# Query, key and value projections by Strassen's seven products over sequence, channel and column halves

## The reference

```python
def dilated_mixer(x, w_qkv, w_o, t5_table):                      # layer A
    qkv = (x @ w_qkv).reshape(B, S, N_DIL, 3, N_HEADS_A, HEAD_DIM)
...
def neighbourhood_mixer(x, w_qkv, w_o, rpb):                     # layer B
    qkv = (x @ w_qkv).reshape(B, rows, GRID_W, 3, H, Dh)
```

## Time and profile before

| | |
|---|---|
| median of 3 runs | 6017.46 us (6017.22 to 6020.44) |
| the profiled execution | 6019.97 us, span of its instructions 6018.3 us |
| TensorE (PE) busy | 5663.1 us, 94% |
| VectorE / ScalarE / POOL busy | 2881.3 / 2306.9 / 1227.2 us |
| mean granted TensorE clock | 0.967 of full speed |
| 16 DMA engines | 212 GB/s mean |

### The profile page before, as it was taken

One profiled execution on the slowest core, in us unless ns is written; L12 is line 12 of the kernel. 1 busy time (PEld: TensorE's weight loads), 2 busy tenths in 40 slices (PEclk: granted clock), 3 DMA queues, 4 the chain that ended last, 5 costly groups with the idle time before them and its releaser, 6 DMA issues. The chain is left out here.

```text
span 6018.3 us, 93104 instructions
## 1 busy us (share of the span) xinstructions
PE 5663.1 (94%) x29818; PEld 4768.2 (79%) x29819; DVE 2881.3 (48%) x5557; ACT 2306.9 (38%) x4179; POOL 1227.2 (20%) x910
## 2 busy tenths in 40 slices
PE   8999999999899997879999979998999896999997
PEld 6888888888799996768887837887999785888773
DVE  3222232222255557675866552322444455755785
ACT  1111111111177775445655411112666213655571
POOL 1331100000000000054755320000000002634673
PEclk9999999999999998979999979999999897999998
DMA  8767744433499987477888574443444325876987
GB/s 252 228 222 234 232 139 138 137 119 119 127 321 316 311 252 209 137 260 261 324 300 297 207 277 153 136 123 118 142 129 136 118 92 183 307 264 224 348 307 276
DMA packets 590506, 1275.30 MB, mean 212 GB/s; under 512 B 39838, under 2 KB 204365, under 8 KB 590220
## 3 DMA queue, kind: packets, MB, share of 16 engines
q1 hardware_dynamic: 398908, 738.28, 36.7%
q0 software_dynamic: 77200, 294.76, 14.1%
q10 hardware_dynamic: 114112, 238.41, 13.1%
HBM read 941.32 MB, written 348.87 MB: 214 GB/s over the span
## 5 line engine op out<-in xcount | busy, mean ns | idle before, releaser
L519 DVE SCALAR_TENSOR_TENSOR qa_stage_lo<-qa_ps_out,qa_stage 128x512 fp32r<-128x512 f32 x192 | 132.5, 690 | 1110.1 <-ACT qa_stage L442 1098.8
L406 PE MATMUL qa_ps_out<-qa_xT_hi,qa_w_hi 128*128 128x512 f32 x1536 | 598.9, 390 | 0.0
L406 PE MATMUL qa_ps_out<-qa_xT_lo,qa_w_hi 128*128 128x512 f32 x1536 | 598.7, 390 | 0.0
L406 PE MATMUL qa_ps_out<-qa_xT_hi,qa_w_lo 128*128 128x512 f32 x1536 | 598.5, 390 | 0.0
L442 ACT ACTIVATE qa_stage<-qa_ps_out 128x512 fp32r<-128x512 f32 x192 | 114.8, 598 | 931.3 <-PE qa_ps_out L406 931.3
L1775 POOL TENSOR_TENSOR a_ex_w_lo<-a_ex_w_raw,a_ex_w_hi 128x1024 fp32r<-128x1024 f32 x128 | 352.8, 2788 | 132.2 <-ACT a_ex_w_hi L1772 127.9
L1775 POOL TENSOR_TENSOR b_ex_w_lo<-b_ex_w_raw,b_ex_w_hi 128x1024 fp32r<-128x1024 f32 x128 | 352.6, 2788 | 129.2 <-ACT b_ex_w_hi L1772 124.6
L794 PE MATMUL da_ps_o<-da_v_two,da_probT 128*128 128x130 f32 x2560 | 355.2, 277 | 0.9 <-DMA da_v_two<-v 0.9
L406 PEld LDWEIGHTS qa_ps_out<-qa_xT_hi,qa_w_hi 128*128 128x128 f32 x1536 | 289.0, 188 | 59.9
L406 PEld LDWEIGHTS qa_ps_out<-qa_xT_hi,qa_w_lo 128*128 128x128 f32 x1536 | 288.9, 188 | 59.9
L406 PEld LDWEIGHTS qa_ps_out<-qa_xT_lo,qa_w_hi 128*128 128x128 f32 x1536 | 288.9, 188 | 59.7
(11 more groups left out here) (429 smaller groups left out, 13811.2 us busy)
## 6 DMA issues: line engine op xcount, KB each, us to landing
a_ex_w_raw<-w SPq DMA_DIRECT2D x128, 1024.0 KB, 12.8
b_ex_w_raw<-w SPq DMA_DIRECT2D x128, 1024.0 KB, 12.4
qa_w_raw<-w_qkv_a SPq DMA_DIRECT2D x36, 2048.0 KB, 9.2
a_ex_w_raw<-w POOLq DMA_DIRECT2D x66, 1024.0 KB, 9.0
b_ex_w_raw<-w POOLq DMA_DIRECT2D x66, 1024.0 KB, 8.8
da_q_cross<-qT SPq DMA_DIRECT2D x48, 1024.0 KB, 9.1
da_k_parts<-kT SPq DMA_DIRECT2D x48, 1024.0 KB, 10.7
ys<-qa_zeros POOLq DMA_DIRECT2D x64, 512.0 KB, 5.8
```

Source lines behind the costliest of these rows:

```text
L406: done = pe.matmul(ps_out[:, j % BANKS, :], stationary, moving, start=first, stop=(k == KC - 1 and m == 2))
L519: dve.scalar_tensor_tensor(out=low.bitcast(F32R), in0=bank, scalar=HD ** -0.5 if kind == 0 else 1.0, in1=high, op0=ALU.mult, op1=ALU.subtr ...
```

## The change

`project_qkv` is rewritten. **A block** is now half of the tokens of both sequences together (512 + 512, a "pass"), a group, a kind and 512 columns; passes are outermost, so 36 blocks in `qa` (2 x 3 x 3 x 2) and 12 in `qb`. In a block, x is a 2 x 2 matrix of (sequence, channel half) blocks and w one of (channel half, column half) blocks, and Strassen's scheme gets the four results from seven products of sums of blocks. A product has 512 tokens, 512 channels and 256 columns. Each product's two banks of PSUM (six in turn) are added into up to two of four partial results in SBUF.

- **x** (28 tiles of a pass, 7 products x 4): SyncE loads one or two 128 x 512 pieces per tile (L398, three tiles in turn), POOL adds or subtracts them (`x_sum`, L359), TensorE turns the sum (`turn`, L460, 4 transposes), ScalarE rounds, VectorE subtracts. In the first pass four tiles stand ready before the first product, and the tiles of product m + 1 are turned between the halves of product m. Those of the second pass are turned during the twelve products around its start.
- **w**: SyncE loads four 512 KB blocks per block (L409, rows of 1 KB), VectorE makes the five sums (`w_sum`, L620) and the low rest (`w_low`, L629), ScalarE rounds (`w_high`, L530), three products ahead.
- **Matmuls**: q and k 24 of 512 columns per product; v 48 of 256 columns.
- **Results**: ScalarE copies products 0, 1, 2 into the partial results (`begin`, L551, 8 copies), VectorE adds (`gather_parts`, L639, 16 of 128 x 512 per block), ScalarE makes the high part of q and k (`finish`, L579, 8) and VectorE the low one (`low_parts`, L690, 8). `stage` and `stage_lo` hold one result per half u, where before each held two banks twice.
- **Stores**: high parts and v by ScalarE (L587, L568), low rests by SyncE (L424). As a pass holds half of a sequence, a row of a store is 512/r tokens: 2 KB for r = 1, 512 B for r = 4, 256 B for r = 8. v has rows of 1 KB.
- **POOL** works on biases after the 28 tiles of pass one; the two mask additions per head move to VectorE (`mask_bias`, L704 and L706, every fourth product from product 48). The 64 zero stores move to pass two, the last after the last product. `bias_rows` now also stores its rows to DRAM and waits for that.

```diff
-        KINDS = [(kind, half) for half in range(2) for kind in range(3)]
-        BANKS = 4
+        W_RING, RAW_RING, BANKS, ROWS = 3, 5, 6, 3
+        X_OF = (((0, 0), (1, 1), 1), ((1, 0), (1, 1), 1), ((0, 0), None, 0), ((1, 0), (0, 0), -1), ((1, 1), None, 0),
+                ((0, 0), (0, 1), 1), ((0, 1), (1, 1), -1))
+        W_OF = (((0, 0), (1, 1), 1), ((0, 0), None, 0), ((0, 1), (1, 1), -1), ((0, 0), (0, 1), 1),
+                ((1, 0), (0, 0), -1), ((1, 1), None, 0), ((1, 0), (1, 1), 1))
+        COMPLETES = (None, None, None, (1, 1), (1, 0), (0, 1), (0, 0))
...
+                def product(p):
+                    n, m = divmod(p, PRODUCTS)
+                    pe.wait_ge(w_lo_done, p + 1)
+                    if n % PER_PASS == 0:
+                        pe.wait_ge(x_lo_done, TILES_OF_PASS * h + 4 * (m + 1))
+                    for u in range(2):
...
+                        for piece in range(1 if kind < 2 else 2):
+                            out = bank if kind < 2 else bank[:, bass.ts(piece, COLS)]
+                            for k in range(KH):
...
+                        for c in tiles_at(2 * p + u):
+                            turn(c)
...
+                        if e >= 2:
+                            act.wait_ge(stored[u], 32 * (e // 2))
...
+                        act.activation(in_class_order(r, stage[:, u, :].bitcast(F32R), True),
+                                       in_class_order(r, result(seq, side, u), False), ACT.Copy, scale=scale_of(kind)
+                                       ).then_inc(high_done, 1)
...
+                            dst = dst.rearrange("c (r i) -> c r i", r=r)[:, :, bass.ts(h, HALF // r)]
+                            act.dma_start(dst, stage[HD * i:HD * i + HD, u, :].rearrange("c (r i) -> c r i", r=r)
+                                          ).then_inc(stored[u], 16)
...
+                for p in range(ALL):
+                    if p + W_RING < ALL:
+                        w_sum(p + W_RING)
+                    for u in range(2):
+                        gather_parts(p, u)
+                        for c in tiles_at(2 * p + u):
+                            x_low(c)
+                    if p + W_RING < ALL:
+                        w_low(p + W_RING)
+                    low_parts(p)
+                    mask_bias(p)
```

More of the change, by code:

```diff
@@ new lines, in project_qkv @@
+        blocks = [(h, g, kind, half) for h in range(PASSES) for g in range(n_g) for kind in range(3) for half in range(2)]
+        PER_PASS = len(blocks) // PASSES
+        ALL = PRODUCTS * len(blocks)
+        TILES_OF_PASS = PRODUCTS * (HALF // P)
+        x_rows = sb("x_rows", [P, ROWS, 2, HALF])
+        x_hi = sb("x_hi", [P, PRODUCTS, KH, HALF], F32R)
+        x_lo = sb("x_lo", [P, PRODUCTS, KH, HALF], F32R)
+        w_raw = sb("w_raw", [P, RAW_RING, KH, COLS])
+        w_whole = sb("w_whole", [P, KH, COLS])
@@ new lines, in project_qkv @@
+        w_hi = sb("w_hi", [P, W_RING, KH, COLS], F32R)
+        w_lo = sb("w_lo", [P, W_RING, KH, COLS], F32R)
+        part = sb("part", [P, 4, 2, HALF])
+        stage = sb("stage", [P, 2, HALF])
+        stage_lo = sb("stage_lo", [P, 2, HALF])
+        ps_x = ctx.enter_context(nc.psum_tensor(f"{tag}_ps_x", [P, 2, KH, P], F32))
+        ps_out = ctx.enter_context(nc.psum_tensor(f"{tag}_ps_out", [P, BANKS, HALF], F32))
+        x_loaded = [sem(f"x_loaded{i}") for i in range(ROWS)]
+        w_loaded = [sem(f"w_loaded{i}") for i in range(RAW_RING)]
@@ new lines, in _ @@
+                for c in range(ROWS):
+                    load_x(c)
+                load_w(0, 0)
+                load_w(0, 1)
+                for c in tiles_at(-1):
+                    load_x(c + ROWS)
+                load_w(0, 2)
+                load_w(0, 3)
+                for n in range(len(blocks)):
+                    if n + 1 < len(blocks):
+                        load_w(n + 1, 0)
+                    for m in range(PRODUCTS):
+                        if m in (2, 4, 5) and n + 1 < len(blocks):
+                            load_w(n + 1, (2, 4, 5).index(m) + 1)
+                        for u in range(2):
+                            for c in tiles_at(2 * (PRODUCTS * n + m) + u):
+                                load_x(c + ROWS)
+                        if m >= 3:
+                            for u in range(2):
+                                store_low(n, m, u)
@@ new lines, in _, with result, in_class_order, scale_of @@
+                for c in tiles_at(-1):
+                    turn(c)
+                for p in range(ALL):
+                    product(p)
+            def result(row, col, u):
+                return part[:, at_result(row, col), u, :]
+            def in_class_order(r, ap, is_stage):
+                if r == 1:
+                    return ap
+                return ap.rearrange("p (r i) -> p r i", r=r) if is_stage else ap.rearrange("p (i r) -> p r i", r=r)
+            def scale_of(kind):
+                return HD ** -0.5 if kind == 0 else 1.0
@@ L510, in low_part @@
-                def low_part(n, j):
-                    s, g, kind, half = chunks[n]
-                    pair, u = j // 2 % 2, j % 2
-                    dve.wait_ge(stage_full, n * OUTS + j + 1)
-                    uses = (lows_before(n) + j) // BANKS
-                    if u == 0 and uses:
-                        dve.wait_ge(lo_stored[pair], 32 * uses)
-                    bank, (high, low) = sorted_views(classes[g], u, pair, ps_out[:, j % BANKS, :], (stage, stage_lo))
-                    dve.scalar_tensor_tensor(out=low.bitcast(F32R), in0=bank, scalar=HD ** -0.5 if kind == 0 else 1.0,
-                                             in1=high, op0=ALU.mult, op1=ALU.subtract).then_inc(lo_full, 1)
@@ new lines, in low_parts @@
+                def low_parts(p):
+                    n, m = divmod(p, PRODUCTS)
+                    h, g, kind, half = blocks[n]
+                    if COMPLETES[m] is None or kind == 2:
+                        return
+                    row, col = COMPLETES[m]
+                    r = classes[g]
+                    for u in range(2):
+                        e = low_units(n) + 2 * (m - 3) + u
+                        dve.wait_ge(high_done, e + 1)
+                        if e >= 2:
+                            dve.wait_ge(lo_stored[u], 32 * (e // 2))
+                        dve.scalar_tensor_tensor(
+                            out=in_class_order(r, stage_lo[:, u, :].bitcast(F32R), True),
+                            in0=in_class_order(r, result(row, col, u), False), scalar=scale_of(kind),
+                            in1=in_class_order(r, stage[:, u, :], True), op0=ALU.mult, op1=ALU.subtract
+                            ).then_inc(low_done, 1)
```

530 lines of the change are left out of this document (305 added, 225 removed).

## The result

The changed kernel takes **5971.6 us** (median of 4 runs, 5968.0 to 5982.1); the kernel before, beside it, 6017.3 (6016.1 to 6020.4). Ratio 0.9926, 95% interval 0.9909 to 0.9943: 46 us faster, where 172 were forecast. The profiled execution took 5971.35 us, 48.6 under that of before.

A forecast was written before the change was run, and what follows sets the result against it. TensorE was taken to bound the qa and qb projections. Terms of -138.3 us in qa and -33.7 in qb, together -172.0 from the profiled 6020.0, gave 5848.0, stated as 5846 us for the median; range 5805 to 5936.

The forecast's parts named there:

- pass switch: Turning pass two's tiles in qa and qb: 28 turns and one wait for the last tile, +19 us each phase.
- Between the phases: Terms outside the blocks: qb's earlier start, -12.3 us, and the last zero store landing after qa, +2.5 us.
- Matmuls and start: Seven products for eight: -177.0 us in qa, -59.0 in qb; first matmul of qa at 34.7 us.
- Tokens beside the products, 10.0 us a product: Block 0 of each phase: products 0 to 5 take 10.0 instead of 5.44 us, +27.4 us a phase.
- 7.8 us for three tiles, 10.4 for four: Block 0's three-deep token-tile ring: issues, landing, sum and turn, giving nearly the same 10.0 us a product.
- Bias transfers, 5 us for each of two blocks: qa's blocks 1 and 2: stores land late beside the bias transfers, +10 us (0 to 24).
- the DMA engines bind in part: Rival: dearer 256 B pieces, or landings over 6 us in more than two blocks; +40 to +90 us, chance 0.13.
- High part 0.598, low rest 0.688 for all classes: Blocks of q and k: us per ScalarE high part and per VectorE 128 x 512 low rest.
- I cost it at nothing; the cover is those 6 us: VectorE in q and k blocks: 31.1 to 34.7 of 38.1 us, hidden with some 6 us to spare.
- VectorE becomes the bound: Rival: VectorE at 42 us a block in 32 q and k blocks, +125 us, 5971 us; chance 0.10.
- Small pieces at 17 ns, 0 us: Stores of q and k with r = 8: 256 B pieces cost 17 ns each, hidden, 0 us.
- The rival that paid twice: r = 8 stores in eight qa blocks: pieces at 56.2 ns, +252 us, 6098 us; chance 0.07.

The follow-up runs named there:

- e1: The change with four instead of three places in qb's ring of token tiles; 5959.1 us, ratio 0.9911.
- e6: The change with every token tile of pass one turned, rounded and subtracted half a product earlier; 5956.3 us, ratio 0.9893.
- e10: The change with SyncE's list reordered, in every product token loads in front of the next block's weight load; 5967.2 us, ratio 0.9921.
- e11: The change with e2, e6, e10, four token-tile places in both phases and the bias transfers as in e9; 5863.8 us, ratio 0.9746.
- e12: e11 with each of the eight diagonal-bias transfers cut in four, one behind each of the first 32 zero stores; 5854.6 us, ratio 0.9729.
- e7: The change with grid-bias transfers one per product from product 8 and the diagonal ones moved into pass two; 6003.1 us, ratio 0.9971.
- e9: As e7, but the eight diagonal-bias transfers stand one by one among pass two's zero stores; 5955.9 us, ratio 0.9900.
- e2: The change with sorting into class order done by copies and additions while reading PSUM; 5939.9 us, ratio 0.9880.

## Why the prediction was wrong

The direction was right, the time 126 us off and outside the range. Three terms of the sum failed: token work beside the products (47 us over both phases), the cost of the bias transfers (31 us) and the price of high parts and low rests (32 us). By the steps of the forecast, for the profiled executions (measured minus forecast, in us):

| step | qa | qb |
|---|---|---|
| start (34.7; 33.4 measured) | -1.3 | in "between" |
| matmuls of 256 columns at 0.120, not 0.118 | +7.8 | +2.6 |
| block 0 (65.5; 89.5 and 88.8) | +24.0 | +23.3 |
| blocks 1 to 3 (+10; +41.3) | +31.3 | |
| strided SBUF, blocks 8 to 16 and 30 to 35 (0; 21.9 and 10.3) | +32.2 | |
| pass switch (+19; 22.3 and 23.4), rest | +4.4 | +4.4 |
| **sum** | **98.4** | **30.3** |

Between the phases -9.8 was forecast (qb's start and the tail) and -16 measured, inside its own spread. 98.4 + 30.3 - 6.3 = 122.4 of the 123.4 us between 5848.0 and 5971.35.

- **Matmuls and start** were right: full clock outside the disturbed blocks, 0.2267 and 0.120 us. The first matmul came at 33.4.
- **Tokens beside the products, 10.0 us a product** failed, as the term of 27.4 a phase measured 51. I took three places as three tiles per pass of the ring ("7.8 us for three tiles, 10.4 for four"), but TensorE turns them in pairs, by the timeline: one is ready when two are wanted (a fourth place: 17 us, e1). The end of a product costs more than 2.5 us (e6), weight loads stand in front of token loads (e10, 8 to 12 us), and behind the longest of these waits TensorE came back at 1.2 GHz, which the sum left out: 8.4 us in qa's block 0. These overlap; with all of them attacked at once, e11 and e12 have block 0 at 60.7 to 62.4, below my 65.5. The term was attainable, not what this order gave.
- **Bias transfers, 5 us for each of two blocks** failed: 41 us in three. I priced only the stores' landings; the weight load, waited for 18.4 us, was not in the sum. e7 and e9 bring the blocks to nominal with the same bytes, spread. The nearest rival is "the DMA engines bind in part", to which I gave 0.13, but its condition was the landing of stores in more than two blocks. In block 3 the stores landed in 3.0 to 3.6 us (medians), and what was late in blocks 1 and 2 was above all the weights, for which it had no term.
- **High part 0.598, low rest 0.688 for all classes** failed, and with it "I cost it at nothing; the cover is those 6 us". Both prices came from rows that read PSUM, the first with the same stride; I carried them to a strided operand in SBUF. VectorE then has 31.1 + 8 x 0.45 = 34.7 us in a block of r = 8 and 38.0 with masks of 3.3 (1.91 us per four products): at TensorE's 38.1. The rival "VectorE becomes the bound" came true in seven blocks of pass one and weakly in four of pass two, by an operand and not by a count; its 5971 us agree with the result by chance. e2 shows it.
- **Small pieces at 17 ns, 0 us** was right, but one of its two grounds was not. The 16.7 ns divide by 28672 rows of the program, while the trace counts 2240 packets of 3.3 KB on average in that queue: they were not moved in pieces of 256 B. The line through 528 B and 2 KB (16.0 ns) is the ground that holds. In 686 to 786 us the queue that moved pieces of 256 B alone had:

```profile
q10 hardware_dynamic: 20592, 5.11, 24.4%
```

0.244 x 100 x 16 / 20592 = 19 ns, less than the 28.1 of 528 B. The rival that paid twice, by my reading of the rule in the Trainium skill ("DMA: Bandwidth & Descriptors", Specifications) that an engine reads, modifies and writes below 512 B, had 56 ns; these stores from SBUF show no such price.

**To carry on.** A ring's depth is worth its depth minus what its reader takes at once, so place takes and refills on one time line before pricing it. Price an operation by the row with the same memory and the same stride, not by the row with the same name. When work is cut finer, ask where each burst on the DMA engines falls, since the loads that feed TensorE share them, and spread it.
